# Second block: where attention waits for stores, which engine splits the dv weights, and the banks of the pooling products

## The reference, cut to what matters

```python
h = rmsnorm(x, norm1_g)
p = h @ w_in                                   # 1024 -> 256 + 3*512 + 3*256
u = p[..., :256]                               # for the pooling mixer
dq, dk, dv = split(p[..., 256:1792], 3)        # differential attention, 4 heads of 2 x 64
sq, sk, sv = split(p[..., 1792:], 3)           # stick-breaking attention, 4 heads of 64
# pooling: 4 groups of 64 channels, trailing mean over 2, 4, 8, 16 positions minus the token,
#          then pooled @ pool_w[g] (64x64), times pool_scale
# differential: (softmax(q1 k1) - lam softmax(q2 k2)) v, causal, headwise rmsnorm
# stick-breaking: A[t,s] = sigmoid(z[t,s]) prod_{s<j<t} (1 - sigmoid(z[t,j])), then A v
x = x + concat(pooling, differential, stick) @ w_out
x = x + (silu(h2 @ w_gate) * (h2 @ w_up)) @ w_down
out = rmsnorm(x, final_norm_g)
```

## Time and profile before

| | us |
|---|---|
| median of 3 runs | 3688.02 (3686.49 to 3693.86) |
| profiled execution | 3687.42 |
| its span | 3685.7 |
| TensorE busy | 3505.6 (95%) |
| VectorE busy | 2130.1 (58%) |
| GpSimd busy | 1732.3 (47%) |
| ScalarE busy | 1155.6 (31%) |

### The profile page before, as it was taken

How to read it: one execution, slowest core, us unless ns; L and a number is a source line. 1 busy time by engine, 2 the same in 40 slices (tenths; PEclk the granted TensorE clock), 3 DMA queues, 4 the chain that set the end, 5 groups by cost and what they waited for, 6 DMA issues and landing times.

```text
span 3685.7 us, 51935 instructions
## 1 busy us (share of the span) xinstructions
PE 3505.6 (95%) x22042; PEld 2927.5 (79%) x22042; DVE 2130.1 (58%) x2745; ACT 1155.6 (31%) x1919; POOL 1732.3 (47%) x1248
## 2 busy tenths in 40 slices
PE   8999999988999999999999999989999899999998
PEld 7788878867778787877878888777788777787876
DVE  7845566377364545456774466647778355454454
ACT  2122122267222222223122122336666222222223
POOL 4332333549255555555233323632488345545454
PEclk9999999999999999999999999999999999999999
DMA  3110312554101111113111132362121200101011
GB/s 124 36 41 30 143 64 83 180 143 143 59 23 46 58 46 58 46 57 143 47 35 35 35 149 80 117 203 70 58 92 58 92 23 35 69 35 69 35 69 63
DMA packets 79690, 275.82 MB, mean 75 GB/s; under 512 B 9057, under 2 KB 9313, under 8 KB 76900
## 3 DMA queue, kind: packets, MB, share of 16 engines
q1 hardware_dynamic: 70816, 242.25, 19.6%
q10 hardware_dynamic: 8642, 30.24, 2.2%
HBM read 224.23 MB, written 48.23 MB: 74 GB/s over the span
## 4 chain that ended last, share of the span: by engine, by line
PE 74%; DVE 15%; ACT 4%; POOL 3%; issue 3%; DMA 0%; POOLq 0%; SPq 0%; DVEq 0%; ACTq 0%
PE ps L1426 20%; PE ps L1428 19%; PE ps L1427 19%; PE ps L1432 4%; PE ps L1726 2%; PE ps L1696 2%; PE ps L1697 2%; PE ps L1731 2%; DVE tf_lo_p L2122 2%; DVE acc L2123 1%; DVE af_hi_p L2122 1%; ACT wd_hi L1780 1%; DVE af_lo_p L2122 1%; DVE px L2122 1%; PE ps L1501 1%
## 5 line engine op out<-in xcount | busy, mean ns | idle before, releaser
L2717 POOL TENSOR_TENSOR ring_lo<-ring_raw,ring_hi 128x512 fp32r<-128x512 f32 (+1 forms) x356 | 596.6, 1681 | 381.8 <-ACT ring_hi L1780 372.2
L1426 PE MATMUL ps<-a_hi,ring_hi 128*128 128x512 f32 x1472 | 589.5, 400 | 29.9 <-DVE af_hi_p L2122 16.0
L1428 PE MATMUL ps<-a_hi,ring_lo 128*128 128x512 f32 x1472 | 575.9, 391 | 0.0
L1427 PE MATMUL ps<-a_lo,ring_hi 128*128 128x512 f32 x1472 | 575.8, 391 | 0.0
L1426 PEld LDWEIGHTS ps<-a_hi,ring_hi 128*128 128x128 f32 x1472 | 277.8, 189 | 104.2 <-DVE af_hi_p L2122 23.6
L1428 PEld LDWEIGHTS ps<-a_hi,ring_lo 128*128 128x128 f32 x1472 | 277.6, 189 | 59.9
L1427 PEld LDWEIGHTS ps<-a_lo,ring_hi 128*128 128x128 f32 x1472 | 278.2, 189 | 54.3
L2122 DVE TENSOR_TENSOR xres<-xres,ps 128x512 f32<-128x512 f32 x352 | 234.6, 684 | 147.9 <-PE ps L1428 145.7
L1426 PE MATMUL ps<-wd_hi,af_hi 128*128 128x512 f32 x704 | 277.0, 394 | 24.5 <-DVE xres L2122 18.7
L1780 ACT ACTIVATE ring_hi<-ring_raw 128x512 fp32r<-128x512 f32 (+1 forms) x286 | 180.6, 635 | 308.8 <-PE ps L1428 195.5
L1427 PE MATMUL ps<-wd_lo,af_hi 128*128 128x512 f32 x704 | 275.8, 392 | 0.0
(11 more groups left out here) (305 smaller groups left out, 8055.6 us busy)
## 6 DMA issues: line engine op xcount, KB each, us to landing
ring_raw<-w SPq DMA_DIRECT2D x92, 512.0 KB, 3.6
ring_raw<-wgu SPq DMA_DIRECT2D x68, 512.0 KB, 3.7
uq<-q_scr SPq DMA_DIRECT2D x96, 256.0 KB, 4.7
ring_raw<-wd SPq DMA_DIRECT2D x34, 512.0 KB, 3.6
ring_raw<-wo SPq DMA_DIRECT2D x32, 512.0 KB, 3.6
uk<-k_scr SPq DMA_DIRECT2D x6, 2048.0 KB, 10.5
rlf<-wgu SPq DMA_DIRECT2D x20, 512.0 KB, 4.5
xraw<-xt SPq DMA_DIRECT2D x16, 512.0 KB, 7.4
```

The costliest lines, as they stand in the source:

```text
L1426: pe.matmul(o, ah, bh, start=begin and i == 0, stop=False)
L1427: pe.matmul(o, ah, bl, start=False, stop=False)
L1428: last = pe.matmul(o, al, bh, start=False, stop=end and i == len(pairs) - 1)
L2717: tt = lambda o, a, b, op: pool.tensor_tensor(o, a, b, op=op)
```

## The change

- The jobs dv00, dv01 and dv11 are split by GpSimd; dv10 stays with ScalarE and VectorE.
- A pair product waits for its first job before the first four row blocks, and for the second job only before the last four. This holds for all pair products of both blocks.
- The pooling products come three turns behind `pool_sum` instead of two, c = 0 and c = 1 in one turn, and in banks 6 and 7.
- The wait of ScalarE and VectorE for the stores from staged tiles moves from the beginning of attention to the beginning of step 3.

```diff
-                job(f"w2{hf}{name}{p}", w2[nb], eng=("act", "dve") if name in ("dv0", "dv1") else ("pool", "pool"),
+                job(f"w2{hf}{name}{p}", w2[nb], eng=("act", "dve") if name + str(p) == "dv10" else ("pool", "pool"),
...
-            env["dense2"] = [("dense", hf, "2dv1", 3), ("pool_lo", hf, 1, 1)] + [m for s in stage + [vst] for m in s.free]
+            env["dense2"] = [("dense", hf, "2dv1", 3), ("pool_lo", hf, 1, 1)]
+            env["spilled"] = [m for s in stage + [vst] for m in s.free]
...
                 emit("pool_sum", hf, j)
-                yield True
-                yield True
+                for _ in range(3):
+                    yield True
                 while ("turned", 1) not in env:
                     yield False
                 for c in range(2):
-                    free = yield from take(BK[6])
+                    free = yield from take(BK[6 + c])
                     emit("pool_mix", hf, j, c, free)
-                    BK[6].free = [("pool_lo", hf, j, c)]
+                    BK[6 + c].free = [("pool_lo", hf, j, c)]
                     env["mix"][j, c] = ("pool_lo", hf, j, c)
-                    yield True
+                yield True
...
+                if x == 3:
+                    emit("attend", hf, env["spilled"])
...
                 if s == 0:
                     for mark in new("pe", free):
                         pe.wait_ge(*at(*mark))
-                    if tp == 0:
-                        for mark in new("pe", [b0["done"], b1["done"]]):
+                tc = slice(256 * tp + 128 * s, 256 * tp + 128 * s + 128)
+                for i, blk in enumerate((b0, b1)):
+                    if tp == s == 0:
+                        for mark in new("pe", [blk["done"]]):
                             pe.wait_ge(*at(*mark))
-                tc = slice(256 * tp + 128 * s, 256 * tp + 128 * s + 128)
-                t = products(PS[b][:, 256 * s:256 * s + 256], [
-                    (XH[:, k, tc], XL[:, k, tc], (b0, b1)[k // 4]["hl"][0][:, 256 * (k % 4):256 * (k % 4) + 256],
-                     (b0, b1)[k // 4]["hl"][1][:, 256 * (k % 4):256 * (k % 4) + 256]) for k in range(8)])
+                    t = products(PS[b][:, 256 * s:256 * s + 256], [
+                        (XH[:, 4 * i + k, tc], XL[:, 4 * i + k, tc], blk["hl"][0][:, 256 * k:256 * k + 256],
+                         blk["hl"][1][:, 256 * k:256 * k + 256]) for k in range(4)], begin=i == 0, end=i == 1)
```

More of the change, by code:

```diff
@@ L1673, in tensor @@
                     z = slice(64 * i, 64 * i + 64)
-                    t = pe.matmul(PS[6][z, :], pc("pool_w")[z, 128 * j + 64 * i:128 * j + 64 * i + 64],
+                    t = pe.matmul(PS[6 + c][z, :], pc("pool_w")[z, 128 * j + 64 * i:128 * j + 64 * i + 64],
                                   PX[1 + i][z, o[i] + 512 * c:o[i] + 512 * c + 512], start=True, stop=True)
@@ L2025, in scalar @@
                         act.wait_ge(*at(*mark))
-                act.activation(AH[:, j, 512 * c:512 * c + 512], PS[6][:, :], ACT.Copy, scale=pc("pool_s", j, 1)).then_inc(
+                act.activation(AH[:, j, 512 * c:512 * c + 512], PS[6 + c][:, :], ACT.Copy, scale=pc("pool_s", j, 1)).then_inc(
                     *up("pool_hi", hf, j, c))
@@ L2625, in vector @@
                         dve.wait_ge(*at(*mark))
-                stt(AL[:, j, cs], PS[6][:, :], pc("pool_s", j, 1), f32(AH[:, j, cs]), ALU.mult, ALU.subtract).then_inc(
+                stt(AL[:, j, cs], PS[6 + c][:, :], pc("pool_s", j, 1), f32(AH[:, j, cs]), ALU.mult, ALU.subtract).then_inc(
                     *up("pool_lo", hf, j, c))
```

## The result

The changed kernel takes 3675.31 us (median of 6 runs, 3672.92 to 3679.37), the kernel before 3688.63 in the same comparison: ratio 0.9962, 95% interval 0.9952 to 0.9972. That is 13 to 14 us faster (10 to 18 by the interval), half of the 26 that I forecast, and outside my range. The profiled execution took 3679.37 us, the slowest of the six; its span is 3677.6, 8.1 us less than that of the profiled execution before.

A forecast was written before the change was run, and what follows sets the result against it. TensorE, busy 95% of the span, was taken as the bound, so only its waits and clock counted. Terms of 13.8 us in hf 0 and 12.2 in hf 1 gave 26.0 off 3687.4: forecast 3661 us, range 3651 to 3673.

The forecast's parts named there:

- Pooling, j = 0: Pooling products issued behind the first sv0 tile pair lose their waits: 6.3 us gained in hf 0, 1.95 in hf 1.
- The clock term: In hf 0, half clock behind the 2.31 us pooling wait goes: 1.7 us of work regained.
- Pooling, j = 1, given back before t4: TensorE's saved waits return before t4; VectorE's shorter chain gains 1.9 us in each half, bounds 0 and 2.8.
- dv0 on GpSimd costs 0: GpSimd's 7 to 10.6 us of splitting dv0 is covered by TensorE's work on u1: cost 0.
- the cheap case: GpSimd's copy and subtraction for a dv0 tile take 3.5 us, against 5.3 in the dear case.
- dv1: TensorE begins product dv1 on dv10 alone: 0.9 us less wait, 0.9 of clock; 1.8 each half (0.3 to 3.0).
- rival (2): VectorE and GpSimd give gains back at t4, dv1 and step 3: gain 17 us, time 3670, chance 0.12.
- Attention, hf 0: Attention begins ahead of the stores' landing, so VectorE's scans start earlier: gain 3.8 us, bounds 2.0 and 5.7.
- rival (3): Attention's start isn't moved, bound by another load or bank: 10.3 us of gain lost, time 3672, chance 0.07.
- Attention, hf 1: First sigmoid comes before the stores land: 4.4 us, plus 2.1 of clock; gain 6.5, bounds 4.4 and 8.5.
- second term, clock and scans: In hf 1's attention, full clock returns as far as VectorE's scans allow, 4 us; half taken, 2.1.
- rival (1): The waits go but the clock doesn't come back, or falls elsewhere: gain 20 us, time 3667, chance 0.20.

The follow-up runs named there:

- e2_pool: Only the pooling products' change (three turns, two banks) on the kernel before; ratio 0.9967 to the kernel before.
- g3_jobs_old: f8_both with the store wait at step 10 and dv0 also back on ScalarE and VectorE; ratio 0.9920 to the kernel before, median 3662.97 us.
- e1_attend: Only the move of the store wait to step 3, on the kernel before; ratio 0.9999 to the kernel before.
- f8_both: Changed kernel with dv11 back on ScalarE and VectorE, dv1's stores behind the second query tile's load, store wait at step 8; ratio 0.9943 to the kernel before, 3669.83 us.
- g2_apart: Changed kernel with GpSimd beginning dv11 only after VectorE's subtraction of dv10 has ended; ratio 0.9956 to the kernel before.
- e4_split_wait: Only the second job's wait moved to the middle of the first tile, on the kernel before; ratio 0.9990 to the kernel before.
- f5_dv11_back: Changed kernel with dv11 split by ScalarE and VectorE again; ratio 0.9950 to the kernel before, median 3671.02 us.
- f7_q_first: f6_step8 with the second query tile's load issued ahead of dv1's two stores; ratio 0.9960 to the kernel before.
- f6_step8: Changed kernel with the wait for the stores at step 8 instead of step 3; ratio 0.9961 to the kernel before.

## Why the prediction was wrong, step by step

- **Pooling, j = 0** (6.3 + 1.95): right, 6.6 and 2.4 us between the marks, with no wait left at the pooling products. The clock term too: in hf 0 the kernel before lost 1.7 us of full-clock work there, the changed one none.
- **Pooling, j = 1, given back before t4** (1.9 each): right in mechanism and size, 2.0 and 1.9; the 2.19 us hole in VectorE's chain is closed, and the t4 wait grew only by 0.85 and 0.2 us (5.98 and 5.31), just under the 6 us that would have spoken against me. The two steps together are e2_pool's 12 us.

```profile
596.30 1.41 DVE L2127 SCALAR_TENSOR_TENSOR a_lo<-ps,par,a_hi 128x512 fp32r<-128x512 f32 x2
```

- **dv0 on GpSimd costs 0**: right; 1.05 + 2.39 us per tile, the cheap case. Nothing waits for it (g3_jobs_old).
- **dv1** (1.8 each): wrong. I had seen the collision and priced it at a third of its size. The wait became 0.1 us shorter, under its lower bound of 0.3, and 2.66 us is outside the 1.5 to 2.3 that I had named as the sign. The full collision, which I had written down as a case (0.3 us and no clock) and as part of rival (2), is what came; for the value I took the middle, although both subtractions start from events that the trace of before fixed within 2 us of each other and must overlap. With 2.66 us left, the half clock stayed too: dv1 to the first scores took 24.6 us in both halves, as before, and 23.1 where the collision was gone. That is 3.4 us of the shortfall.
- **Attention, hf 0** (3.8, bounds 2.0 to 5.7): wrong, it failed below its lower bound. The step that failed is that only ScalarE's wait for the stores held the first steps. I followed ScalarE, VectorE and the banks, and not the load that stands behind the stores in SyncE's queue; before, it landed 1.9 us ahead of its use, so it was the next bound. My rival (3) had the mechanism, "another load", but I argued it away with the wait's releaser, which tells what is late now and nothing of what is late next. It won 1.1 us up to scores 8, and 2.6 were lost again behind them, at half clock that the kernel before did not have there. 5.3 us of the shortfall.
- **Attention, hf 1** (6.5 in the sum of two terms): right within its bounds, 5.4 measured between dv1 and the mark, 6.3 in e1_attend. TensorE's wait is 2.23 us instead of 6.62, as worked out, and none is ended by the query tile. The second term, clock and scans, was partly there: the full-clock work lost from the first scores to the mark went from 6.8 to 5.1 us. In f8_both none was lost there, and the stretch took 48.7 us, where it was 56.9 before and 51.5 in the changed kernel.

```profile
2446.39 0.60 PE L1700 MATMUL ps<-uk,uq 128*128 128x512 f32 x1 [2.23 <-ACT rowa L2042]
...
2449.38 0.80 PE L1700 MATMUL ps<-uk,uq 128*128 128x512 f32 x1 [0.66 <-ACT rowa L2042]
```

- **The clock elsewhere**: rival (1) had named it, but the sum leaves it out. "Everything else of TensorE is as before" held for its instructions and not for its clock. 26.0 less 3.4, 5.3 and 1.1 is about 16; the medians say 13.3, interval 10 to 18. The two profiled executions differ by 8.1 us, and the changed one lost about 8 us more of full-clock work over the whole span. Both together are 16 again, an estimate, since clock that is lost while TensorE waits costs nothing. Whether the change makes half clock more frequent elsewhere stays open. The profiles give a hint, one execution of each kernel: from hf 1's last mark to the end, seven of the nine kernels with the moved store wait lost 16.1 to 16.5 us (the other two, g2_apart and g3_jobs_old, 13.1 and 11.8), the four without it 9.8 to 13.7. e1_attend is one of the seven.

My range was too narrow since I added the bounds of single terms (the upper ones make 34, not 35), and two of these bounds were wrong in themselves: in hf 0 the bound left out a resource, and at dv1 the collision, which had to come, cost a little more than its lower bound allowed. The other terms of the sum (pooling, 12.1 of 26 us, and attention in hf 1) had mechanism and size right.

## What to carry to other kernels

When a wait is taken away at a seam between two stages, list every transfer that is issued at that seam and write down how long before its use it lands now; the smallest of these margins bounds what can be won up to that use, whatever the waiting engine gains. Work moved to GpSimd beside a VectorE operation with two SBUF inputs should be priced at the collided duration on both sides when the starting events of both are near each other. And a wait that moves behind a transfer must be moved again whenever that transfer moves.

## What the runs showed of the hardware

- VectorE's subtraction of 128 x 1024 fp32 tiles in SBUF took 1.23 us alone (g2_apart) and 2.26 beside GpSimd's of the same shape (changed kernel), which took 2.92 instead of 2.40. The Trainium skill (GPSIMD Engine Reference, Key points) says that GpSimd shares its SBUF interfaces with VectorE, with contention for VectorE instructions that have two SBUF inputs, as this one has; the trace agrees.
- A wait of TensorE of 1.62 us before dv1 left the granted clock at 1.00 (e4_split_wait, f5_dv11_back); with 2.66 us there the row behind it shows 0.60, a part of it at half clock. So the last 1.04 us of that wait cost another 1.5 us behind it (24.6 instead of 23.1 us from dv1 to the first scores).
- The four loads of the second query tile, 256 KB each, took 6.4 us (median, from issue to landing) behind 1 MB of stores in the changed kernel, and 4.7 us ahead of them in f7_q_first, where the stores took 9.2 us instead of 3.4. Their consumer started 3.3 us earlier than in f6_step8: the last of the four was issued 2.3 us earlier (2.2 instead of 4.5 us after the first scores) and landed 1.0 us faster.
